# Weight loads ahead of bias rows, a compressed bias made on TensorE, the gate product on GpSimd, and first products ordered by contraction row, in a ten-stage fp32 network kernel

## The reference

```
for layer in (0, 1):
    x = x + 0.5 * swiglu(norm(x))            # ffn1_0, ffn1_1
    x = x + mixer(norm(x))                   # pooling, Fourier, differential attention
    x = x + 0.5 * swiglu(norm(x))            # ffn2_0, ffn2_1, final norm
then sparse attention (nsa), MoE (moe_0), a gated recurrence (hgrn), MoE (moe_1)
nsa:  bias[q, k] = table[bucket(q - k)]      # relative bias, 16 heads
      compressed scores use bias at one key position in 16
      x = x + gate * (attention(...) @ w_out)
moe:  x = x + gate * (weight_0 * expert_a + weight_1 * expert_b)
```

## Time and profile before

| | us |
|---|---|
| median of 3 runs | 3506.87 (3504.22 to 3514.69) |
| the profiled execution | 3497.12 |
| its span | 3495.3 |
| mean granted TensorE clock | 0.964 |

### The profile page before, as it was taken

How to read it: one execution, slowest core, us unless ns; L and a number is a source line. 1 busy time by engine, 2 the same in 40 slices (tenths; PEclk the granted TensorE clock), 3 DMA queues, 4 the chain that set the end, 5 groups by cost and what they waited for, 6 DMA issues and landing times. The chain is left out here.

```text
span 3495.3 us, 40219 instructions
## 1 busy us (share of the span) xinstructions
PE 3260.8 (93%) x15458; PEld 2605.5 (75%) x15458; DVE 2040.7 (58%) x2660; ACT 1438.8 (41%) x1946; POOL 155.5 (4%) x191
## 2 busy tenths in 40 slices
PE   7999998999999999998999969788999879999995
PEld 6888776788878888757888858545688658877884
DVE  4554426545545553354554445354788768868886
ACT  4222225322232222353222132264588646646884
POOL 0000000000000000000000000242000000001000
PEclk9999999999999999999999989799999989999998
DMA  5332230333223321341332141300799731119995
GB/s 200 127 144 108 101 108 3 151 138 144 108 91 145 144 109 53 139 115 79 138 156 114 60 150 37 73 1 25 299 419 416 286 120 61 61 52 396 417 415 211
DMA packets 96872, 534.19 MB, mean 153 GB/s; under 512 B 18816, under 2 KB 19712, under 8 KB 48336
## 3 DMA queue, kind: packets, MB, share of 16 engines
q1 hardware_dynamic: 85488, 491.24, 36.8%
q0 software_dynamic: 6624, 24.12, 1.8%
q10 hardware_dynamic: 4608, 16.78, 1.2%
HBM read 508.95 MB, written 32.06 MB: 155 GB/s over the span
## 5 line engine op out<-in xcount | busy, mean ns | idle before, releaser
L453 ACT ACTIVATE ffn_silu_gate<-ffn_gate_up 128x512 f32<-128x512 f32 x88 | 52.6, 598 | 960.3 <-PE ffn_gate_up L117 960.3
L515 DVE TENSOR_TENSOR ffn_product<-ffn_silu_gate,ffn_gate_up 128x512 f32<-128x512 f32 x88 | 60.5, 688 | 558.5 <-ACT ffn_silu_gate L453 558.5
L2620 DVE TENSOR_TENSOR moe_low<-moe_raw,moe_high 128x2048 fp32r<-128x2048 f32 x144 | 326.5, 2286 | 30.8 <-ACT moe_high L2537 30.7
L115 PE MATMUL ffn_down<-ffn_down_high,ffn_hid_high 128*128 128x512 f32 x704 | 282.6, 401 | 1.5 <-DVE x_tok L539 1.3
L539 DVE SCALAR_TENSOR_TENSOR x_tok<-ffn_down,x_tok 128x512 f32<-128x512 f32 x352 | 232.8, 687 | 82.6 <-PE ffn_down L117 81.2
L116 PE MATMUL ffn_down<-ffn_down_low,ffn_hid_high 128*128 128x512 f32 x704 | 281.0, 399 | 0.0
L117 PE MATMUL ffn_down<-ffn_down_high,ffn_hid_low 128*128 128x512 f32 x704 | 280.4, 398 | 0.0
L115 PE MATMUL ffn_gate_up<-ffn_h_high,w 128*128 128x512 f32 x704 | 280.2, 398 | 0.0
L116 PE MATMUL ffn_gate_up<-ffn_h_low,w 128*128 128x512 f32 x704 | 278.4, 395 | 0.0
L2537 ACT ACTIVATE moe_high<-moe_raw 128x2048 fp32r<-128x2048 f32 x144 | 274.2, 1917 | 9.9 <-PE moe_bank L117 9.9
L117 PE MATMUL ffn_gate_up<-ffn_h_high,w 128*128 128x512 f32 x704 | 278.2, 395 | 0.0
(11 more groups left out here) (609 smaller groups left out, 7174.0 us busy)
## 6 DMA issues: line engine op xcount, KB each, us to landing
moe_raw<-in_moe_w SPq DMA_DIRECT2D x192, 1024.0 KB, 8.3
ffn_raw_gate_up<-in_ffn_gate_up SPq DMA_DIRECT2D x85, 1024.0 KB, 6.3
ffn_ada_w<-in_ada_w SPq DMA_DIRECT2D x32, 1536.0 KB, 7.1
ffn_raw_down<-in_ffn_down SPq DMA_DIRECT2D x88, 512.0 KB, 3.4
mixer_w_raw<-in_mix_w SPq DMA_DIRECT2D x22, 1024.0 KB, 5.2
hgrn_w_raw<-in_hgrn_w SPq DMA_DIRECT2D x19, 1024.0 KB, 5.2
moe_y<-moe_y ACTq DMA_DIRECT2D x32, 512.0 KB, 9.4
nsa_w_raw<-in_nsa_w SPq DMA_DIRECT2D x13, 1024.0 KB, 5.6
```

Source lines behind the costliest of these rows:

```text
L115: pe.matmul(out, lhsT[0], rhs[0], start=first, stop=False)
L453: act.activation(silu_gate[slot][:, :], gate_up_ps[2 * slot][:, :], ACT.Silu).then_inc(silu_done, 1)
L515: dve.tensor_tensor(product[slot][:, :], silu_gate[slot][:, :], gate_up_ps[2 * slot + 1][:, :], ALU.mult)\
L2620: dve.tensor_tensor(low[n % SPLITS][:, :, :], raw[n % RAWS][:, :, :], high[n % SPLITS][:, :, :].bitcast(FP32), ALU.subtract)\
```

## The change

Three things are changed.

1. **First products by row.** In ffn (all four), in `project` with a norm (mixer_0, mixer_1, nsa) and in hgrn the first product runs over rows k outside and tiles inside. A row's turn (`norm.turn_next`) comes behind the matmuls of all tiles of the row before it.
2. **nsa.** Weight loads 3 and 4 are issued ahead of the wait for the bias rows, load 5 ahead of `bias_copies`. The gate row is loaded by DMA from `mod_rows`, which mixer_0's SP list stores. The compressed bias is made by 31 small matmuls (banks `CBIAS`) from the buckets, which are twice as long, and the wait for `strip` moves down to the fused scores.
3. **MoE tail.** POOL multiplies by the gate row; DVE does tile t's weighing before tile t-1's addition.

```diff
@@ ffn
+            def first_gate_up():
+                for k in range(KT):
+                    norm.row(pe, k)
+                    for m in range(2):
+                        last = gate_up_product(0, m, k)
+                    norm.turn_next(pe, k)
                 last.then_inc(gate_up_done, 1)
...
-            gate_up(0, 0, False)
+            first_gate_up()
@@ project
+        if norm is not None:
+            w_high, w_low = self.take(pe, 2 * group)
+            banks = [self.banks.open(pe, o + m) for m in range(4)]
+            for k in range(4):
+                norm.row(pe, k)
+                for m in range(4):
+                    last = self.product(pe, banks[m], m, k, w_high, w_low, high, low, token_major)
+                norm.turn_next(pe, k)
+            last.then_inc(self.half_used, 1)
+            norm.row(pe, KT - 1)
+        for half in range(norm is not None, 2):
@@ hgrn
+            def first_part():
+                for k in range(4):
+                    norm.row(pe, k)
+                    for m in range(4):
+                        last = product(0, m, k)
+                    norm.turn_next(pe, k)
+                last.then_inc(half_used, 1)
+                norm.row(pe, KT - 1)
@@ nsa, SP
+            weights.fill(sp, 3, 5)
             banks.wait_for(sp, ROWS)
             banks.wait_for(sp, ROWS + 1)
             sp.dma_start(dram["bias_rows"], rows).then_inc(rows_stored, 16)
+            weights.fill(sp, 5, 6)
             sp.wait_ge(rows_stored, 16)
...
             sp.dma_start(dram["bias_copies"], one).then_inc(rows_stored, 16)
-            weights.fill(sp, 3, 10)
+            weights.fill(sp, 6, 10)
...
+            sp.wait_ge(chip.mod_rows_stored[0], 48)
+            sp.dma_start(gate_row[:, :], dram["mod_rows"][0, 2].unsqueeze(0).broadcast_to([P, DM])).then_inc(gate_loaded, 16)
@@ nsa, PE
-            pe.wait_ge(diag_ready, 1)
             for a in range(2):
-                bank = banks.open(pe, GROW[a])
-                for k in range(4):
-                    last = pe.matmul(bank[:, k * P:(k + 1) * P], chip.ones[:, :], diag[:, 4 * a + k, :],
+                bank = banks.open(pe, CBIAS[a])
+                for n in range(16 * a, min(16 * a + 16, NCMP)):
+                    at = 640 + 481 - 16 * n
+                    last = pe.matmul(bank[:, NH * (n % 16):NH * (n % 16) + NH], buckets[:, at:at + P], table[:, :],
                                      start=True, stop=True)
@@ nsa, DVE
-            dve.wait_ge(strip_loaded, 16)
...
+                                        row_halves[:, :, half, :, 24 - 8 * i:24 - 8 * i + NB[i]]))
...
+            dve.wait_ge(strip_loaded, 16)
             fused_scores(0)
@@ MoE tail, POOL and DVE
+            for t in range(TT):
+                pool.wait_ge(summed, t + 1)
+                pool.tensor_tensor(pair[t][:, 1, :], pair[t][:, 1, :], gate_row[:, :], ALU.mult).then_inc(gated, 1)
...
-                dve.wait_ge(summed, t + 1)
...
-                dve.tensor_tensor(pair[t][:, 1, :], pair[t][:, 1, :], gate_row[:, :], ALU.mult).then_inc(gated, 1)
...
+                if t > 0:
+                    add(t - 1)
+            add(TT - 1)
```

More of the change, by code:

```diff
@@ L384, in gate_up @@
             def gate_up(n, slot, again=True):
-                first = not again and slot == 0
-                if not first:
-                    pe.wait_ge(gu_ready, n)
+                pe.wait_ge(gu_ready, n)
                 if again:
@@ L391, in gate_up, with gate_up_product @@
                     for k in range(KT):
[L392 to L398, removed]
+                        last = gate_up_product(slot, m, k)
+                last.then_inc(gate_up_done, 1)
+            def gate_up_product(slot, m, k):
+                return split_matmul(pe, gate_up_ps[2 * slot + m][:, :], (gu_high[slot][:, m, k, :], gu_low[slot][:, m, k, :]),
+                                    (norm.high[:, k, :], norm.low[:, k, :]), k == 0, k == KT - 1)
+            def first_gate_up():
[4 more added lines that the diff above has]
+                    norm.turn_next(pe, k)
                 last.then_inc(gate_up_done, 1)
@@ L796, in project, with product, halves @@
     def project(self, pe, group, o, high, low, token_major, norm=None):
-        for half in range(2):
-            for _ in self.halves(pe, group, half, o, high, low, token_major, norm):
-                pass
-    def halves(self, pe, group, half, o, high, low, token_major, norm=None):
+        if norm is not None:
[9 more added lines that the diff above has]
+        for half in range(norm is not None, 2):
+            for _ in self.halves(pe, group, half, o, high, low, token_major):
+                pass
+    def product(self, pe, bank, m, k, w_high, w_low, high, low, token_major):
+        at, i = slice(m * P, (m + 1) * P), k % 4
+        if token_major:
+            return split_matmul(pe, bank[:, :], (high[:, k, at], low[:, k, at]), (w_high[:, i, :], w_low[:, i, :]), k == 0, k == KT - 1)
+        return split_matmul(pe, bank[:, :], (w_high[:, i, at], w_low[:, i, at]), (high[:, k, :], low[:, k, :]), k == 0, k == KT - 1)
+    def halves(self, pe, group, half, o, high, low, token_major):
         w_high, w_low = self.take(pe, 2 * group + half)
@@ L808, in halves @@
             bank = self.banks.open(pe, o + m) if half == 0 else self.banks.ps[(o + m) % self.banks.n]
-            at = slice(m * P, (m + 1) * P)
             for i in range(4):
[L811 to L821, removed]
+                last = self.product(pe, bank, m, 4 * half + i, w_high, w_low, high, low, token_major)
             if half == 1:
@@ L1939, in _ @@
             norm.turn_first(pe)
+            first_part()
             for gi in range(FIRST):
-                for half in range(2):
+                for half in range(gi == 0, 2):
                     for m in range(4):
@@ L2892, in _, with add @@
         def _(dve):
+            def add(t):
+                dve.wait_ge(gated, t + 1)
+                dve.tensor_tensor(chip.x[:, t, :], chip.x[:, t, :], pair[t][:, 1, :], ALU.add).then_inc(x_added, 1)
             for t in range(TT):
@@ L2975, in constants @@
     f = np.float32
[L2976 removed]
+    return {"moe_const": moe.astype(f), "hgrn_masks": masks, "hgrn_keep": keep, "nsa_buckets": np.concatenate([distance_buckets(), distance_buckets()[:, ::-1]], 1), "mix_near": near.astype(f), "mix_dft": dft.astype(f), "chan_dft": chan.astype(f), "alibi": alibi.astype(f)}
 def distance_buckets():
```

55 lines of the change are left out of this document (22 added, 33 removed).

## The result

The changed kernel takes 3512.9 us (median of 15 runs) against 3500.8 (15 runs), ratio 1.0027 with a 95% interval of 1.0018 to 1.0037. It is 0.27% slower, some 9.5 us (6 to 13 by the interval; the medians differ by 12.1), where 6 us less was forecast. The forecast's 3501 was reckoned from a median of three runs, 3506.9; from the 3500.8 of 15 runs the same change would have been 3495. Of all runs of the experiments one, of the kernel with turns ahead, took 5087 us at a granted clock of 0.604 and enters no ratio. The profiled execution took 3514.3 us.

What follows compares the result with a forecast made beforehand. PE, busy 3260.8 of 3495.3 us, was taken as the bound, so only its waits could be saved. The terms -20.6 - 10.4 - 3.4 + 25.7 + 2.5 gave -6.2 us, 3491 profiled and 3501 as median, range 3488 to 3516.

Steps and rivals of the forecast that it cites:

- A: First products in mixer_0, mixer_1, nsa, hgrn: PE stalls 19.5 us, slow starts 6.2; +25.7 us, bounds +19.5 to +27.
- B: nsa weight loads: the 19.07 us wait for a weight half goes, with 1.55 of slow clock; -20.6 us.
- C: nsa compressed scores' softmax no longer waits for `strip` and starts with PE's scores; -10.4 us, bounds -8 to -10.4.
- D: nsa compressed bias: 31 narrow matmuls take 5.2 us in place of 2.7; +2.5 us, bounds +1 to +3.6.
- E: MoE tails: POOL's product runs beside DVE's work; -2.1 and -1.3, together -3.4 us, bounds -5 to +1.
- rival 1: MoE tails: DVE and POOL don't run side by side, 3.5 us later a tail; 3511 us, chance 0.28.
- faster: Whole kernel: chance that the change comes out faster, put at 0.21, beside same 0.65 and slower 0.14.
- Rival 2: First products: PE's idle time there doesn't bring the half clock; 3494 us, chance 0.10.
- Rivals 3, 4 and 5: First-product stalls smaller or absent, 3475 (0.07); nsa weight split late, 3521 (0.09); `strip` late, 3504 to 3509 (0.10).

Runs made afterwards that it cites:

- kernel with turns ahead: Changed kernel with its MoE tail on DVE and each row's turn issued ahead of that row's matmuls; ratio 0.9974 against the kernel before.
- the pairing experiment: The nsa part alone, its 31 narrow matmuls alternating between two halves of the rows and two banks; 3471.4 us, 0.9929 against the kernel before.
- the memset: Changed kernel with POOL's product in the MoE tails replaced by a memset of the same tile; single run, 3837.7 us.

## Why the prediction was wrong

**The sum by its own steps.** The parts measured alone are by row +0.68%, tail +0.27%, nsa -0.60%, together +0.35%, against 0.27% for the whole: they add up within their intervals.

- **A, first products by row, +25.7.** Right in place and in the stalls, mis-sized in the clock. From a stage's first transposes to its second half PE takes 5.5, 5.0, 5.3 and 4.3 us more than before (mixer_0, mixer_1, nsa, hgrn), 20.0 where 19.5 was forecast. In hgrn the stall itself is whole, and the removed row waits show ahead of it: the stretch took 18.42 us (2815.87 to 2834.29) and takes 22.75 (2821.55 to 2844.30). That it fits so well there is partly luck: with the tail on DVE the same list takes 24.43 us, with its first matmuls at the half clock. The step that failed is the price of a slow start. The forecast took 1.55 from the two stretches of the earlier trace rows, at whose ends the half clock was over; behind the mixers' new stalls it went on for 5.6 us and more. The four cost 9.8 us where 6.2 was forecast, and 8.1 and 7.9 in two other kernels with these stalls (tail on DVE, by row alone). In the traces of all three kernels A comes to 29.7 to 29.9 us, above its bound of 27; the runs of the kernel by row alone say 24, with an interval of 18 to 29.
- **B, weight loads, -20.6.** Right: alone it is -23 with an interval of -27 to -18.
- **C, strip, -10.4.** Right: 17.34 to 6.92 in PE's wait, DVE's step of 7.05 came as 7.06.
- **D, narrow matmuls, +2.5.** Mis-sized: 10.4 us for 2.7, +7.7, beyond the bound of +3.6. The step took 0.17 us for each of 31 matmuls, from the 11.43 us of the earlier trace rows at up to 0.18. Those are 64 matmuls in 128 records, 0.09 a record, that alternate between the two halves of the rows and between banks, and the pairing experiment shows that such alternation halves the price. The changed kernel's own matmuls all stand on rows 0 to 63 and take 0.168 a record, two records a matmul.
- **E, tails, -3.4.** Wrong in sign: +4.1 in each. The step that failed is the one that let DVE weigh and add beside POOL's product. That was rival 1, which had 0.28 and a price of +3.5 a tail; 4.1 came; POOL's first product also waits for its last fetch to be issued (it starts at 2800.46, 0.8 us behind the end of DVE's first weighing), which is about the difference. The Trainium skill's page SBUF — State Buffer, section Who interferes with whom, gives the rule with its condition, two SBUF inputs on DVE against a POOL operation that reads SBUF. The traces agree on both halves of it: 3.37 us beside the product, 1.28 beside the memset. It deserved the larger chance: the kernel before had nothing against it, and the forecast gave the overlap the benefit of the doubt. This one term turned the sign: with -3.4 replaced by +8.2 alone the sum is +5.4.

With D and E corrected the sum is -6.2 + 5.2 + 11.6 = +10.6 us, which looks like the 9.5 that was measured, but by luck: with A at the 29.8 of its trace it is +14.7, which is 5 us above what the runs say and 2 above their interval (6 to 13). That rest stays unexplained. In the chances, the weights named for "faster" add up to 0.19, not 0.21; nothing hangs on it. The profiled spans differ by 16.9, more than the runs: mixer_0, with ffn1_0 alone ahead of it, starts at 404.42 in place of 400.31, behind a stretch of narrow matmuls whose clock was 0.63 and 0.50 (380 to 390) where before it was 1.00 and 0.73 (376 to 386); that start lies between 400.6 and 405.4 across the experiments, whatever the edit. So a single pair of spans can't tell less than these 5 us. Without the 4.1 us ahead of mixer_0 the spans differ by 12.8.

**The rivals.** Rival 1 happened. Rival 2 (a stall without the half clock) is out at 5 us and true at 2.2 us. Rivals 3, 4 and 5 are out: the stalls are whole, the weights' wait is gone, `strip` was in time. What stays open is why one slow start costs 2.9 us and another 1.4 (mixer_0 in the changed kernel and in the one with its tail on DVE, each behind a stall of 4.99 us), and why the runs say 24 us for A where the traces say 30.

**What was best.** The nsa part with paired narrow matmuls, 0.9929, beats both kernels: 25 us faster than before, 34 faster than the changed one. The runs can't tell it from the three moved loads alone (0.9935) or from the nsa part with ffn by row (0.9930).

## What to carry to other kernels

A loop order that gives each row more work also delays what is issued at a row's end; look who queues behind the last of these (here the rounding of the next weights), and issue it ahead of the row's work. Before a product is moved from VectorE to GpSimd, ask what VectorE does beside it: in this tail, where both read two SBUF tiles, nothing overlapped, and the slower engine's time simply replaced the faster one's. Read the price of a fallen clock from how long the same matmuls take at full clock and behind the stall, until they are done, not from one stretch of the profile. In a change of several parts measure each alone: here three moved lines gave as much as the whole part that gained.

## What was not expected of the hardware

- A DVE row's length beside a POOL operation includes the time in which it was shut out (3.37 for 1.28), and the other way round (3.27 for some 2.2). Busy shares of both engines then overstate their work: POOL's went from 155.5 to 179.8 us for eight products.
- Narrow fp32 matmuls of 64 rows and 16 columns take 0.18 us a record at the half clock and 0.11 at the full one on one half of the rows and one bank, and 0.097 and 0.054 when alternated between the halves and two banks.
- PE's clock fell to 0.50 while PE was busy all the time with those narrow matmuls (window 2110 to 2114), not only behind idle time.
- Stalls of 2.2 and 2.3 us left the clock at 1.00, stalls of 5.0 and 5.1 brought it to 0.50. Behind these the same 48 matmuls took from 1.4 to 3.0 us longer.
